# Where the parts of the next block's input are made at six joints of a two-block transformer kernel

## The reference

```python
def first_block(x, norm_gains, ...):
    for layer in range(DEPTH):                       # DEPTH = 2
        g = norm_gains[layer]
        h = rmsnorm(x, g[0])
        x = x + 0.5 * rmsnorm(swiglu(h, ...first...), g[1])
        h = rmsnorm(x, g[2])
        x = x + rmsnorm(token_mixer(h, ...), g[3])
        h = rmsnorm(x, g[4])
        x = x + 0.5 * rmsnorm(swiglu(h, ...second...), g[5])
    return x
```

## Time and profile before

| | |
|---|---|
| median of three runs | 3649.42 us (3646.39 to 3652.32) |
| profiled execution, its own time | 3652.75 us |
| its span | 3651.0 us |
| TensorE busy | 3487.0 us (96%), mean granted clock 0.983 |
| VectorE busy | 1679.9 us (46%) |
| ScalarE busy | 1271.5 us (35%) |
| GpSimd busy | 1402.8 us (38%) |
| waits of TensorE for the first high part, six joints of block 1 | 22.4 us |

### The profile page before, as it was taken

The page is one execution under the profiler, slowest core; times in us unless marked ns, Lnnn a source line. Parts: engine busy times, 40 slices in busy tenths (PEclk is TensorE's granted clock), DMA queues, the critical chain, the costliest instruction groups (busy, mean ns, idle before and its releaser), DMA issues. The chain is left out here.

```text
span 3651.0 us, 44956 instructions
## 1 busy us (share of the span) xinstructions
PE 3487.0 (96%) x16100; PEld 2743.6 (75%) x16100; DVE 1679.9 (46%) x2602; ACT 1271.5 (35%) x2154; POOL 1402.8 (38%) x599
## 2 busy tenths in 40 slices
PE   8999999999999999998999999899999899999998
PEld 6888766688878887766888777567888776568886
DVE  5441354644254424356443346864331539753313
ACT  3222356422232223365222342453222442642223
POOL 3444321344434443321444334313444345124443
PEclk9999999999999999999999999999999999999999
DMA  4333311233322333211333231102333320113332
GB/s 174 98 96 95 115 58 35 75 98 95 98 84 92 98 96 112 75 47 47 98 98 98 82 122 54 47 19 86 98 95 96 110 76 29 41 53 98 97 93 98
DMA packets 86330, 308.01 MB, mean 84 GB/s; under 512 B 11157, under 2 KB 11669, under 8 KB 84798
## 3 DMA queue, kind: packets, MB, share of 16 engines
q1 hardware_dynamic: 86206, 306.37, 26.3%
HBM read 301.59 MB, written 4.74 MB: 84 GB/s over the span
## 5 line engine op out<-in xcount | busy, mean ns | idle before, releaser
L329 POOL TENSOR_TENSOR wL<-ring,wH 128x1024 fp32r<-128x1024 f32 x519 | 1264.8, 2437 | 2130.1 <-ACT wH L319 2033.4
L281 PE MATMUL bank<-hH,wH 128*128 128x512 f32 x2448 | 964.2, 394 | 10.9 <-DVE yT L756 4.8
L283 PE MATMUL bank<-hH,wL 128*128 128x512 f32 x2448 | 953.8, 390 | 0.0
L282 PE MATMUL bank<-hL,wH 128*128 128x512 f32 x2448 | 953.4, 389 | 0.0
L319 ACT ACTIVATE wH<-ring 128x1024 fp32r<-128x1024 f32 (+1 forms) x525 | 551.0, 1050 | 1125.2 <-PE bank L283 938.0
L281 PEld LDWEIGHTS bank<-hH,wH 128*128 128x128 f32 x2448 | 460.0, 188 | 115.7 <-issue 6.1
L283 PEld LDWEIGHTS bank<-hH,wL 128*128 128x128 f32 x2448 | 459.8, 188 | 97.3
L282 PEld LDWEIGHTS bank<-hL,wH 128*128 128x128 f32 x2448 | 460.3, 188 | 93.7 <-issue 1.4
L281 PE MATMUL bank<-guH,wH 128*128 128x512 f32 x1248 | 491.7, 394 | 2.3 <-ACT early L1152 1.4
L283 PE MATMUL bank<-guH,wL 128*128 128x512 f32 x1248 | 486.4, 390 | 0.0
L282 PE MATMUL bank<-guL,wH 128*128 128x512 f32 x1056 | 410.8, 389 | 0.0
(11 more groups left out here) (285 smaller groups left out, 4072.7 us busy)
## 6 DMA issues: line engine op xcount, KB each, us to landing
ring<-in_w SPq DMA_DIRECT2D x376, 512.0 KB, 3.5
ring<-in_down SPq DMA_DIRECT2D x96, 448.0 KB, 3.2
ring<-in_down SPq DMA_DIRECT2D x48, 512.0 KB, 3.4
ring<-in_next SPq DMA_DIRECT2D x16, 512.0 KB, 3.4
mix<-in_table SPq DMA_DIRECT2D x2, 2560.0 KB
mix<-spread SPq DMA_DIRECT2D x4, 768.0 KB, 5.5
mix<-row SPq DMA_DIRECT2D x1, 2560.0 KB
spread<-mix SPq DMA_DIRECT2D x1, 2560.0 KB, 7.7
```

What stands on the lines that cost most here:

```text
L281: eng.matmul(out, a, hi, start=first, stop=False)
L282: eng.matmul(out, a, lo, start=False, stop=False)
L283: return eng.matmul(out, b, hi, start=False, stop=last)
L329: eng.tensor_tensor(l[:, 0:width], ring[:, n % NSLOT, 0:width], h[:, 0:width], ALU.subtract).then_inc(w_lo, 1)
```

## The change

The low part of h moves from VectorE to GpSimd (pool_parts, placed in GpSimd's queue ahead of the weight parts that follow). GpSimd subtracts hH from a copy of x scaled by the gain, which ScalarE makes for it in a buffer of two halves (sq), so each chunk on ScalarE is high part, scaled copy, square. The copy for chunk m waits until GpSimd is done with chunk m - 2. The inverse root is written to bank 4 (after all copies of y), and the scaled output to banks 5 and 6 in turns, not in place; scaled waits for the x of two chunks before. VectorE does scaled of the next chunk ahead of moved. The high part of the third slot goes ahead of the root in ScalarE's queue. In pair_of, at every place where it is used, the two low products of a chunk come after the four high products of the next.

```diff
--- before.py
+++ after.py
@@ -229,6 +229,7 @@
         hsq = sem("hsq")
         hsum = sem("hsum")
         hrs = sem("hrs")
+        z_made = sem("z_made")
         hout = sem("hout")
         hmix = sem("hmix")
         silu_g = sem("silu_g")
@@ -390,16 +391,40 @@
             eng.wait_ge(ln_ready, q + 1)
             eng.activation(rs, lnv, ACT.Exp, scale=-0.5).then_inc(rs_ready, 1)
 
-        def act_split(eng, xr, gains, squares, third=None):
-
+        post_rs = bank[4][:, :]
+
+        def act_post_root(eng, q, r, third):
+
+            hi(eng, third)
+            eng.wait_ge(stat_ready, q + 1)
+            eng.activation(lnv, bank[6][:, :], ACT.Ln, bias=EPS_RMS).then_inc(ln_ready, 1)
+            eng.wait_ge(ln_ready, q + 1)
+            eng.wait_ge(y_done, 8 * r + 8 + 2)
+            eng.activation(post_rs, lnv, ACT.Exp, scale=-0.5).then_inc(rs_ready, 1)
+
+        def act_parts(eng, xr, gains):
 
             for m in range(KD):
-                if third is not None and m == KD - 1:
-                    hi(eng, third)
-                if xr is None:
-                    eng.wait_ge(x_in[m // 2], 16 if m // 2 else 32)
-                else:
-                    eng.wait_ge(x_ready, xr + m + 1)
+                g = gains[:, m:m + 1]
+                eng.wait_ge(x_ready, xr + m + 1)
+                eng.activation(hH[:, m, :], xT[:, m, :], ACT.Copy, scale=g).then_inc(h_hi, 1)
+                if m >= 2:
+                    eng.wait_ge(h_ready, xr + 8 + m - 1)
+                eng.activation(sq[:, m % 2, :], xT[:, m, :], ACT.Copy, scale=g).then_inc(z_made, 1)
+                eng.activation(yT[:, m, :], xT[:, m, :], ACT.Square).then_inc(xsq_ready, 1)
+
+        def pool_parts(eng, xr):
+
+            for m in range(KD):
+                eng.wait_ge(h_hi, xr + 8 + m + 1)
+                eng.wait_ge(z_made, xr + m + 1)
+                eng.tensor_tensor(hL[:, m, :], sq[:, m % 2, :], hH[:, m, :], ALU.subtract).then_inc(h_ready, 1)
+
+        def act_split(eng, gains, squares):
+
+
+            for m in range(KD):
+                eng.wait_ge(x_in[m // 2], 16 if m // 2 else 32)
                 if gains is None:
                     eng.activation(hH[:, m, :], xT[:, m, :], ACT.Copy).then_inc(h_hi, 1)
                 else:
@@ -418,16 +443,15 @@
 
         def scaled(eng, n, m, g):
 
-            eng.scalar_tensor_tensor(yT[:, m, :], yT[:, m, :], g[:, m:m + 1], rs,
+            if m >= 2:
+                eng.wait_ge(x_ready, n + m - 1)
+            eng.scalar_tensor_tensor(bank[5 + m % 2][:, :], yT[:, m, :], g[:, m:m + 1], post_rs,
                                      ALU.mult, ALU.mult).then_inc(t_ready, 1)
 
-        def moved(eng, n, m, b):
+        def moved(eng, n, m):
 
             eng.wait_ge(t_ready, n + m + 1)
-            if b is None:
-                eng.tensor_tensor(xT[:, m, :], xT[:, m, :], yT[:, m, :], ALU.add).then_inc(x_ready, 1)
-            else:
-                eng.tensor_scalar(xT[:, m, :], yT[:, m, :], b[:, m:m + 1], None, ALU.add).then_inc(x_ready, 1)
+            eng.tensor_tensor(xT[:, m, :], xT[:, m, :], bank[5 + m % 2][:, :], ALU.add).then_inc(x_ready, 1)
 
         def vector_lo(eng, n):
 
@@ -436,36 +460,37 @@
             h, l = parts_of(n)
             eng.tensor_tensor(l, ring[:, n % NSLOT, :], h, ALU.subtract).then_inc(w_lo, 1)
 
-        def dve_post(eng, q, n, g, third, h0=None, gains=None, b=None):
+        def dve_post(eng, q, n, g, third):
 
 
             eng.wait_ge(rs_ready, q + 1)
             scaled(eng, n, 0, g)
-            for m in range(KD + 1):
-                if m < KD:
-                    moved(eng, n, m, b)
+            for m in range(KD):
                 if m + 1 < KD:
                     scaled(eng, n, m + 1, g)
-                if m >= 1 and h0 is not None:
-                    rest(eng, h0, m - 1, gains)
+                moved(eng, n, m)
             vector_lo(eng, third)
 
 
         def pair_of(eng, n, h0, banks=(0, 2)):
 
             landed(eng, n + 1)
-            for kc in range(KD):
-                two = [(bank[b][:, :], *(v[:, kc * P:(kc + 1) * P] for v in parts_of(n + u)))
-                       for u, b in enumerate(banks)]
-                eng.wait_ge(h_hi, h0 + kc + 1)
-                for out, a, b in two:
-                    eng.matmul(out, a, hH[:, kc, :], start=(kc == 0), stop=False, skip_group_check=True)
-                    eng.matmul(out, b, hH[:, kc, :], start=False, stop=False, skip_group_check=True)
-                eng.wait_ge(h_ready, h0 + kc + 1)
-                for out, a, b in two:
-                    mm = eng.matmul(out, a, hL[:, kc, :], start=False, stop=(kc == KD - 1), skip_group_check=True)
-                    if kc == KD - 1:
-                        mm.then_inc(slots_done, 1)
+            def two(kc):
+                return [(bank[b][:, :], *(v[:, kc * P:(kc + 1) * P] for v in parts_of(n + u)))
+                        for u, b in enumerate(banks)]
+
+            for kc in range(KD + 1):
+                if kc < KD:
+                    eng.wait_ge(h_hi, h0 + kc + 1)
+                    for out, a, b in two(kc):
+                        eng.matmul(out, a, hH[:, kc, :], start=(kc == 0), stop=False, skip_group_check=True)
+                        eng.matmul(out, b, hH[:, kc, :], start=False, stop=False, skip_group_check=True)
+                if kc:
+                    eng.wait_ge(h_ready, h0 + kc)
+                    for out, a, b in two(kc - 1):
+                        mm = eng.matmul(out, a, hL[:, kc - 1, :], start=False, stop=(kc == KD), skip_group_check=True)
+                        if kc == KD:
+                            mm.then_inc(slots_done, 1)
 
         def pe_ffn(eng, c, n0, h0, free, stat=None, norm=None):
 
@@ -624,7 +649,6 @@
 
             act_silu(eng, c, n0, q, third)
             act_down(eng, n0 + 2 * KF, lambda m, i, per: act_y(eng, r, n0 + 2 * KF, 3, m, i, per))
-            act_root(eng, q + 1, EPS_RMS)
 
         def pool_ffn(eng, n0):
             pool_silu(eng, n0)
@@ -1278,7 +1302,7 @@
                 act.preload_act_table_set(EXP_LN)
                 hi(act, 0)
                 hi(act, 1)
-                act_split(act, None, gnext, True)
+                act_split(act, gnext, True)
                 hi(act, 2)
 
             @block.vector
@@ -1354,8 +1378,9 @@
                 @block.scalar
                 def _(act):
                     act_ffn(act, 0, 0, n_ffn0, 0)
+                    act_post_root(act, 1, 0, n_in + 2)
                     act.wait_ge(par_in, 64)
-                    act_split(act, 0, gcol[:, 16:24], True, n_in + 2)
+                    act_parts(act, 0, gcol[:, 16:24])
                     act_hi(act, n_in + 3, 1)
                     act_root(act, 2, EPS_RMS)
                     act.activation(rlog, bank[3][:, 0:NT], ACT.Ln, bias=EPS_RMS).then_inc(r_steps, 1)
@@ -1368,10 +1393,11 @@
                     act_soft(act)
                     act_stick(act)
                     act_out1(act)
-                    act_root(act, 3, EPS_RMS)
-                    act_split(act, 8, gcol[:, 32:40], True, n_ffn1 + 2)
+                    act_post_root(act, 3, 1, n_ffn1 + 2)
+                    act_parts(act, 8, gcol[:, 32:40])
                     act_ffn(act, 1, 2, n_ffn1, 4, third=True)
-                    act_split(act, 16, gnext, True, n_next + 2)
+                    act_post_root(act, 5, 2, n_next + 2)
+                    act_parts(act, 16, gnext)
 
                 @block.vector
                 def _(dve):
@@ -1391,7 +1417,7 @@
                     dve.wait_ge(bias_out, 16)
                     dve_ffn(dve, 0, n_ffn0, True)
                     dve_ys(dve, 0)
-                    dve_post(dve, 1, 0, ghalf[:, 8:16], n_in + 2, 8, gcol[:, 16:24])
+                    dve_post(dve, 1, 0, ghalf[:, 8:16], n_in + 2)
                     sum_x_squares(dve, 1)
                     vector_lo(dve, n_in + 3)
                     dve.wait_ge(rs_ready, 3)
@@ -1409,21 +1435,24 @@
                     dve_soft(dve)
                     dve_stick(dve)
                     dve_out1(dve)
-                    dve_post(dve, 3, 8, gcol[:, 24:32], n_ffn1 + 2, 16, gcol[:, 32:40])
+                    dve_post(dve, 3, 8, gcol[:, 24:32], n_ffn1 + 2)
                     sum_x_squares(dve, 2)
                     vector_lo(dve, n_ffn1 + 3)
                     dve.wait_ge(rs_ready, 5)
                     dve_ffn(dve, 1, n_ffn1, True)
                     dve_ys(dve, 2)
-                    dve_post(dve, 5, 16, ghalf[:, 40:48], n_next + 2, 24, gnext)
+                    dve_post(dve, 5, 16, ghalf[:, 40:48], n_next + 2)
 
                 @block.gpsimd
                 def _(pool):
                     pool_ffn(pool, n_ffn0)
+                    pool_parts(pool, 0)
                     los(pool, n_in + 2, n_out + 2)
                     pool_diff(pool)
                     los(pool, n_out + 2, n_ffn1 + 2)
+                    pool_parts(pool, 8)
                     pool_ffn(pool, n_ffn1)
```

(1 more changed line is left out.)

## The result

The changed kernel takes 3655.57 us (median of 20 runs, 3648.01 to 3663.09) against 3650.68 for the kernel before (20 runs, 3646.39 to 3657.0). The ratio is 1.0014, with a 95% interval of 1.0007 to 1.002: a slowdown of 0.14%, too small to call slower by the bound of 0.2%, but clear of zero. The prediction was 3654.7. Its profiled execution has a span of 3652.8 us and a time of 3654.58.

A forecast was written before the change was run, and what follows sets the result against it. TensorE, busy 96% of the span, was taken as paced by VectorE at the six joints. Two layers of +2.4 each plus +0.5 in block 2 gave +5.3 us, from 3649.42 to 3654.7 us; range 3649 to 3663.

The forecast's parts named there:

- The sum: Six joints (block output becoming the next block's normalised input): +4.8 over two layers; block 2 +0.5; in all +5.3 us.
- The root's delay: Joints 1 and 3: logarithm queued behind the third slot's load and high part, 1.67 and 1.64 us later; joint 2 nothing.
- VectorE's order: Start of each joint: scaled 1 ahead of the first x moves the first high part 0.43 to 0.53 us later, taken 0.5.
- ScalarE's pace: Chunks at a joint: ScalarE replaces VectorE as the pace, 1.78 us a chunk instead of 1.93.
- 1.05 over seven: Chunks at a joint: gain from the shorter pace, 0.15 us a chunk, 1.05 over seven.
- the unknown: VectorE's scaled with a bank also as output: in no row, cost between 0 and 0.37 us a chunk, all hidden.
- The pair's end: Block 1 joints: pair of slots ends at T + 15.8 us against 15.75, T being the first high part's start.
- Block 2: pair_of's two more matmuls behind the last high part: 0.25 us at each of block 2's two ends, +0.5 in all.
- A: Rival at the root: third slot's data is there in time or scheduling hides it; -1.3 us, 3648.1; chance 0.08.
- B: Rival at joints: ScalarE's chunk exceeds 1.78 us, by waits or TensorE's clock staying at 1.2 GHz; 3661; chance 0.19.
- C: Rival at joints: VectorE's two new forms collide with GpSimd, 2.7 us a chunk, 6.4 a joint; 3693; chance 0.05.
- D: Rival: faster by over 0.2%, needing 1.2 us less at each of six joints; chance 0.04.

The follow-up runs named there:

- e1: The changed kernel with the third slot's high part behind the root's exponential instead of ahead of its logarithm; 3647.5 us.
- e5: The kernel before with one edit, the third slot's high part ahead of the root; 3661.8 us, ratio 1.0027.
- e2: The changed kernel with VectorE's first x ahead of the second scaled, as before; 3650.95 us, ratio 0.9997.
- e4: The changed kernel with root and scaled output in SBUF again while GpSimd makes the low parts; 3671.22 us, one run.
- e7_last_on_vector: The changed kernel with chunk 7's low part on VectorE and no scaled copy of chunk 7 on ScalarE; 3656.28 us.
- e10_last_unordered: The changed kernel with third high part behind root, first x first, low products right behind high, chunk 7's low part on VectorE without waiting for GpSimd; 3645.7 us.

## Why the prediction was right, point by point

- The sum, +5.3: joints and block 2 hold +4.3, the medians +4.9. The forecast 3654.7 against 3655.57, in the case it was put in (within 0.2%, slower by a little). That the time fits to 0.9 us is in part luck: it starts from the median of three runs, 3649.42, which 20 runs put at 3650.68, 1.3 higher, and the sum was 1.0 too high by the joints.
- The root's delay, forecast 1.67 at joint 1 and 1.64 at joint 3: it was 1.75 and 1.73 in layer 0, 1.54 and 1.62 in layer 1. ScalarE's wait for the load was 2.00 and 1.98 us at the two in layer 0, and at joint 2 0.41 with the logarithm on time 0.28 behind it, where I had said ScalarE would be done before it was due. Undone (e1) and done alone (e5), it weighs 1.24 to 1.47 and 1.51 to 1.70. Right.
- VectorE's order, 0.5: by e2 0.78 against 1.32 us from scaled to x, 0.54. Right. The rule of the Trainium skill that I had set against it (VectorE: DVE Perf Modes, "The DRAIN you can't avoid": a semaphore between VectorE operations costs nothing extra, as measured there on copies) doesn't hold here: two operations of these forms start 0.66 apart without a dependence and 0.78 with one (386.00 - 385.22). The rule would have made the step 0.66, some 0.7 us over six joints, too little to show in the medians; e2's rows decide against it.
- ScalarE's pace, 1.78 a chunk: it is 1.75, for a high part whose engine has not waited costs its follower 0.61 to 0.62, not 0.63. Small as it is, over seven chunks it is 0.2 us, and it is most of why joint 2 gained 0.94 instead of 0.73 and joint 1 lost 0.62 to 0.86 instead of 0.94. The mechanism was right, the term a little large. One figure beside the sum was wrong: "1.05 over seven". In the kernel before the last high part began 13.06 to 13.12 us after the first and not seven times 1.93, because VectorE has no low part to make between the first two x. So the pace gave 0.81 to 0.88; the sum, which counts from the first high part, does not use the figure.
- GpSimd's subtraction at 1.28: it is 1.29. VectorE's two forms with a bank among the inputs: 0.748 to 0.756 and 0.678 to 0.682 over all 48 of each, with a bank as output too. 29 and 36 of them ran beside a GpSimd operation. No collision, and the unknown (the bank as output) costs 0.01.
- The pair's end at T + 15.8: 15.61 to 15.63. Joint 3 +2.2: 2.14 and 2.04.
- Block 2, +0.5: 0.25 at its middle, and 0.45 at the last pair, of which 0.25 reach the end of the program. Why not all of the 0.45 gets there (VectorE's low part ends almost as late, by the prediction) was not tested apart.
- The rivals. A is out by the load's rows. B: the pace did not slip. TensorE's clock has no say at a joint: it rose 3.5 to 6.1 us after the pair's first matmul in the changed kernel, and 5.3 to 6.3 us in the kernel before, where at joint 1 of layer 1 it had not fallen at all; and the pair's end stands 15.61 to 15.63 us after the first high part in the one, and at 15.75 at both joints 1 in the other, with and without the fall. C is out; e4 shows that its price was set too high as well, by the argument under that run. D did not come about.
- Not foreseen: that VectorE's third low part would hold GpSimd back by 0.34 us was in the text with up to 1.3, and hidden as said. That the root's wait for the last copy of y costs 0.3 once the delay ahead of it is gone was missed, because the delay hid it in the sum.

So the answer to why five edits that each relieve something gave a slower kernel: the pace went from 1.93 to 1.75 us a chunk, and the last high part came 0.8 to 0.9 us sooner after the first. Where the pair's end counts, 0.7 of that was spent on a longer tail (copy, GpSimd, two matmuls). Where the reduction counts (joints 1 and 2), it was kept, with 0.7 more because the third slot's parts no longer stand there. VectorE's new order cost 0.5 at all six. And a step put ahead of the root, for a slot that nobody was waiting for, cost 1.2 to 1.7 us at four of them.

## What to carry to other kernels

Before a step is moved earlier in an in-order queue, look for the landing time of what it reads: here it needed data that landed 0.7 us after the engine was due elsewhere, while 2 us of idle time stood open just behind. When a chain of equal chunks is relieved by another engine, count the pace and the tail apart: the pace is won once per chunk, the tail is paid once, and which of the two the end hangs on can differ from joint to joint. For edits of a tenth of a per cent, take the shifts of the same instruction in both traces; they repeat to 0.2 us where medians of 11 runs stand up to 4 us off.

## What the runs showed of the hardware

**The clock's share in the spread.** Both kernels vary between 3646 and 3663 us from run to run. In the 20 runs of the changed kernel time and mean granted clock go together (correlation -0.93): the two fastest, 3648.01 and 3649.36, have 0.985 and 0.986, the slowest, 3663.09, 0.981; by a line through them a thousandth of clock is worth 2.5 us (1.2 to 2.5 in the 11 runs of each of the others). One place where it arises is in the mixer, where TensorE stands 2.40 us for VectorE in both kernels. In the kernel before the matmuls behind that wait ran at 1.2 GHz, in the changed one at 2.4; of the twelve profiled executions, one of each kernel here, six fell at this wait and six did not:

```profile
463.12 0.80 PE L281 MATMUL bank<-hH,wH 128*128 128x512 f32 x1 [2.40 <-DVE yT L756]
463.71 0.63 PE L282 MATMUL bank<-hL,wH 128*128 128x512 f32 x1
464.14 0.63 PE L283 MATMUL bank<-hH,wL 128*128 128x512 f32 x1
```
```profile
464.33 0.50 PE L282 MATMUL bank<-hH,wH 128*128 128x512 f32 x1 [2.40 <-DVE yT L780]
464.67 0.40 PE L283 MATMUL bank<-hL,wH 128*128 128x512 f32 x1
464.90 0.39 PE L284 MATMUL bank<-hH,wL 128*128 128x512 f32 x1
```

The changed kernel stood 1.21 us behind the other before this stretch and 0.19 ahead of it at 466 us, so it gained 1.4 here, and by the same reading some 1.0 to 1.3 around 590 us; in block 2's mixers the shift moved by -1.8 in one layer and by +2.1 in the other (there the cause was not followed place by place). Such shifts, of the size of a joint's, are what stands between the +4.3 of the joints and the 1.8 us by which the two profiled spans differ. Whether a shift of a joint by a microsecond changes how often TensorE falls to the lower clock is open. The mean clocks of 11 runs go from 0.9823 (e5_third_alone, joints +6.1) to 0.9847 (e1_root_first, -1.2), in the direction of the time lost at joints and further apart than the scatter of the single runs makes likely. But e7_last_on_vector (+2.1) has 0.9824 and e10_last_unordered (-5.9) 0.9832, so the order is not that of the joints, and no run here isolates it.

**Two engines that hold each other.** VectorE with two SBUF inputs against GpSimd: 0.68 becomes 1.77 us and 1.28 becomes 1.83 when both have work (e4_no_banks), 2.68 at worst beside a GpSimd subtraction of 2.4. With one input in a bank nothing was lost at any of the 96 operations, 65 of them beside GpSimd; the reduction, with one input, took 7.47 to 7.51 us at joints 1 and 2, beside GpSimd's last part, against 7.37 to 7.40 before.
